# Expert-choice layer: full-precision tokens gathered per pair of experts, with four one-time places for expert 0's down weights

## The reference, cut to what matters

```python
def expert_choice_moe(xn, w_router, w_gate, w_up, w_down):
    cap = EC_CAPACITY_FACTOR * T // N_EXPERTS          # 32 tokens for each of 16 experts
    aff = jax.nn.softmax((xn @ w_router).astype(jnp.float32), axis=-1)
    g, idx = lax.top_k(jnp.swapaxes(aff, 1, 2), cap)
    xs = xn[bidx, idx]                                 # 32 x 1024 for each expert
    hid = jax.nn.silu(jnp.einsum('becd,edf->becf', xs, w_gate)) * jnp.einsum('becd,edf->becf', xs, w_up)
    y = jnp.einsum('becf,efd->becd', hid, w_down) * g[..., None].astype(xn.dtype)
    return jnp.zeros_like(xn).at[bidx, idx].add(y)
```

## Time and profile before

| what | us |
|---|---|
| device time, median of 3 runs | 2300.64 |
| lowest, highest | 2297.3, 2301.79 |
| profiled execution: its span, first to last instruction (the only time that its page gives) | 2299.6 |
| PE busy, PEld busy | 1914.4, 1382.4 |
| DVE busy, ACT busy, POOL busy | 913.0, 508.0, 30.6 |

### The profile page before, as it was taken

The page is one execution under the profiler, slowest core; times in us unless marked ns, Lnnn a source line. Parts: engine busy times, 40 slices in busy tenths (PEclk is TensorE's granted clock), DMA queues, the critical chain, the costliest instruction groups (busy, mean ns, idle before and its releaser), DMA issues.

```text
span 2299.6 us, 30109 instructions
## 1 busy us (share of the span) xinstructions
PE 1914.4 (83%) x13228; PEld 1382.4 (60%) x13228; DVE 913.0 (40%) x1242; ACT 508.0 (22%) x517; POOL 30.6 (1%) x23
## 2 busy tenths in 40 slices
PE   7999999999999999999999997556556665666565
PEld 7998789999999889999768672111111111111112
DVE  6788468556678647654346630000000000000001
ACT  4554023333455212333231120000000000000001
POOL 0000000000000010000000000000000000000000
PEclk9999999999999999999999979888887778788887
DMA  7444625556544634556524259999999999999996
GB/s 262 161 147 147 247 75 189 186 158 190 184 147 147 233 125 143 160 176 170 197 83 146 88 219 424 427 427 428 428 428 428 428 428 428 428 428 428 428 427 268
DMA packets 190182, 613.21 MB, mean 267 GB/s; under 512 B 8252, under 2 KB 106044, under 8 KB 164796
## 3 DMA queue, kind: packets, MB, share of 16 engines
q1 hardware_dynamic: 187712, 602.04, 67.7%
q10 hardware_dynamic: 2364, 9.58, 1.1%
HBM read 610.55 MB, written 1.05 MB: 266 GB/s over the span
## 4 chain that ended last, share of the span: by engine, by line
PE 53%; DMA 36%; DVE 8%; ACT 1%; issue 1%; SPq 0%; DVEq 0%; ACTq 0%; PEldq 0%
DMA work<-in_w_down 13%; DMA work<-in_w_gate 11%; DMA work<-in_w_up 11%; PE PS L1694 8%; PE PS L1687 8%; PE PS L1689 8%; PE PS L687 5%; PE PS L1621 3%; PE PS L925 2%; DVE ring_low L2396 1%; PE PS L941 1%; PE PS L1603 1%; PE PS L1717 1%; PE PS L1711 1%; PE PS L1712 1%
## 5 line engine op out<-in xcount | busy, mean ns | idle before, releaser
L925 PE MATMUL PS<-work,proj 128*32 128x512 f32 x1024 | 153.6, 734 | 99.0 <-DMA work<-in_w_up 64.3
L1449 DVE TENSOR_TENSOR proj<-proj,PS 128x512 f32<-128x512 f32 x16 | 11.0, 687 | 488.8 <-PE PS L925 488.8
L925 PE MATMUL PS<-ring,proj 128*32 128x512 f32 x768 | 116.1, 733 | 86.0 <-DMA ring<-in_w_up 49.9
L2147 ACT ACTIVATE high_f<-ring 128x4096 fp32r<-128x4096 f32 (+1 forms) x38 | 120.8, 3178 | 220.9 <-PE PS L1694 209.9
L2379 DVE TENSOR_TENSOR ring_low<-ring,high_f 128x4096 fp32r<-128x4096 f32 (+1 forms) x38 | 146.8, 3863 | 53.5 <-ACT high_f L2147 53.5
L925 PEld LDWEIGHTS PS<-work,proj 128*32 128x32 f32 x1024 | 31.1, 122 | 212.9 <-DMA work<-in_w_up 102.3
L1687 PE MATMUL PS<-xh_f,high_f 128*128 128x256 f32 x640 | 153.6, 280 | 0.3
L1689 PE MATMUL PS<-hT_low,high_f 128*128 128x256 f32 x624 | 151.1, 283 | 0.0
L687 PE MATMUL PS<-hT,ring 128*128 128x256 f32 (+1 forms) x576 | 130.4, 386 | 1.2 <-ACT hT L1068 1.2
L941 PE MATMUL PS<-work,proj 128*32 128x512 f32 x496 | 86.4, 831 | 49.8 <-DMA work<-in_w_down 46.4
L925 PEld LDWEIGHTS PS<-ring,proj 128*32 128x32 f32 x768 | 22.9, 121 | 172.6 <-DMA ring<-in_w_up 79.7
(11 more groups left out here) (527 smaller groups left out, 3702.6 us busy)
## 6 DMA issues: line engine op xcount, KB each, us to landing
ring<-in_w_in SPq DMA_DIRECT2D x73, 1024.0 KB, 7.3
work<-in_w_gate SPq DMA_DIRECT2D x33, 2048.0 KB, 35.7
work<-in_w_up SPq DMA_DIRECT2D x31, 2048.0 KB, 35.6
work<-in_w_down SPq DMA_DIRECT2D x31, 2048.0 KB, 35.7
ring<-in_w_up SPq DMA_DIRECT2D x25, 2048.0 KB, 35.6
ring<-in_w_gate SPq DMA_DIRECT2D x23, 2048.0 KB, 36.0
ring<-in_w_down SPq DMA_DIRECT2D x22, 2048.0 KB, 35.7
ring<-in_w_ada SPq DMA_DIRECT2D x24, 1024.0 KB, 7.3
```

The lines of the kernel that those rows point to most:

```text
L925: mm = nt.matmul(PS[32 * j:32 * j + 32, 2 + n // 4, :], x(k), w[:, F_E * kk + 512 * j:F_E * kk + 512 * (j + 1)], start=(k == 0), stop=(k = ...
L2147: na.activation(high(n)[:, w], ring[:, n % RING, w], ACT.Copy).then_inc(high_ready, 1)
```

## The change

Three things are changed together.

1. **Tokens.** They are kept once, in full 32-bit precision (TOK, written by the same four ACT instructions as `tok_high` before). `low_tokens` and its four DVE instructions are gone.
2. **Gather.** Only the 64 chosen places of a pair of experts are gathered at a time: 16 matmuls of 128 x 64 for each pair, all into bank 2, and one DVE addition over 128 x 512 (new `stage`) that writes XS of the pair. The first pair's gather stands ahead of expert 0; each later one stands on PE in the odd expert before it, between the turning of the hidden values and the down slots. PICK is rebuilt for each pair by two DVE comparisons of 128 x 64 from ROW, a copy of the row of token numbers. The ACT additions into XS (L1170) and the per-expert copies of DVE (L1439) are gone. All four zeroed bank pairs are opened in `route`, between the last turned tokens and the L898 matmul.
3. **Places.** The smaller tiles free blocks of `proj`, and `lora` and its neighbours are laid directly behind it. Expert 0's four down slots now each have a one-time place: `extra_a` (issued after `cat_ready` 1), `extra_b` (after `u2_ready` 4), the two halves in `con` and `hT` as before, and `extra_c` (after `ix_ready`). The ring's eight places hold its slots 0 to 7. The ring's own loads start again at m = 12, when PE has consumed expert 0's slot 0, and m = 20 waits for expert 1's slot 0.

The silu, product and result tiles share buffers (HE, YE on HSE; YE2 on HTE), and the squares of the router's norm use half the room. The numbers of the SP list after the first pair, the loop, the last expert's halves and everything behind them stay as they were.

The diff, cut to its core:

```diff
-PAIR, EXTRA = 2, 8
+PAIR, EXTRA, EXTRAS = 2, 8, 4
...
+        extra_a = proj[:, 8:24, :].rearrange("p a b -> p (a b)")
+        extra_b = nc.alloc_sbuf_tensor_at("extra_b", [P, SLOT], F32, offset=place["proj"] + 4 * 49 * T)
+        extra_c = proj[:, 33:49, :].rearrange("p a b -> p (a b)")
+        extra_halves = (con[:, 256:256 + SLOT // 2], hT[:, :, :].rearrange("p k t -> p (k t)"))
         def turn(m):
-            return m - 1
+            return m - EXTRAS
         def first_slot(m):
-            return m + 1 if m < EXTRA else m
+            return m + EXTRAS if m < EXTRA else m
...
+            first_load(0)
+            sp.wait_ge(block_done, BASE2 + 16)
+            first_load(1)
+            sp.wait_ge(cat_ready, 1)
+            sp.dma_start(extra_a, first_down(0).rearrange(whole, r=4)).then_inc(extra_a_full, 16)
+            sp.wait_ge(u2_ready, 2 * TT)
+            sp.dma_start(extra_b[:, :], first_down(1).rearrange(whole, r=4)).then_inc(extra_b_full, 16)
+            sp.wait_ge(yt_ready, 4)
+            for n in (2, 3, 4):
+                first_load(n)
+            sp.wait_ge(r_ss, 2)
+            first_load(5)
+            sp.wait_ge(block_done, BASE2 + 18)
+            first_load(6)
+            sp.wait_ge(block_done, BASE2 + 20)
+            first_load(7)
+            w = first_down(2).rearrange("(p h r) n -> h p (r n)", h=2, r=2)
+            for half, dst in enumerate(extra_halves):
+                sp.dma_start(dst, w[half]).then_inc(con_loaded, 16)
+            sp.wait_ge(ix_ready, 1)
+            sp.dma_start(extra_c, first_down(3).rearrange(whole, r=4)).then_inc(extra_c_full, 16)
+            for m in range(EXPERT_SLOTS, PAIR * EXPERT_SLOTS):
+                earlier = m - RING_E - EXTRAS if m < RING_E + EXPERT_SLOTS else m - RING_E
+                sp.wait_ge(expert_slots, EXPERT_SLOTS + earlier + 1)
+                sp.sem_inc(slot_freed, 1)
+                expert_load(m // EXPERT_SLOTS, m % EXPERT_SLOTS, m)
...
-                pe.wait_ge(topk_done, 1)
                 pe.wait_ge(dve2, 4)
-                zero_banks(YB[2:3])
+                zero_banks(YB[2:4])
+                pe.wait_ge(tok2_out, 4)
+                zero_banks(YB[0:2]).then_inc(scattered, 1)
                 pe.wait_ge(diag_ready, 1)
                 nt.matmul(PS[:, 3, :], ones[0:EXPERTS, :], DIAG[0:EXPERTS, :], ...).then_inc(row_ready, 1)
...
-                pe.wait_ge(tok2_low, 4)
+            def gather(first):
+                for k in range(KD):
+                    for t in range(TT):
+                        if first and k == 0:
+                            pe.wait_ge(pick_ready, t + 1)
+                        mm = nt.matmul(PS[:, 2, PAIR * CAP * k:PAIR * CAP * (k + 1)], TOK[:, t, 2 * P * (k // 2) + k % 2:2 * P * (k // 2 + 1):2],
+                                       PICK[:, t, :], start=(t == 0), stop=(t == TT - 1))
+                mm.then_inc(xs_psum, 1)
...
             def expert(e, pair, par):
-                pe.wait_ge(xs_staged, e)
+                if par == 0:
+                    pe.wait_ge(xs_out, pair + 1)
                 for n in range(8):
-                    hidden(staged, pair, EXPERT_SLOTS * par + n)
+                    hidden(staged(par), pair, EXPERT_SLOTS * par + n)
+                turned(e)
+                if par:
+                    pe.wait_ge(pick_ready, pair + 4)
+                    gather(False)
                 rest(e, pair, par)
             def first_expert():
-                gather(0, 4)
+                gather(True)
                 pe.wait_ge(ix_out, 1)
-                for n in range(4):
-                    if n in (1, 2):
-                        gather(2 * n + 2, 2 * n + 4)
-                    pe.wait_ge(xs_out, 2 * n + 2)
-                    hidden(first, 0, first_slot(n), n)
-                for n in range(4, 8):
-                    hidden(first, 0, first_slot(n), n)
-                zero_banks(YB[3:4] + YB[0:2]).then_inc(scattered, 1)
-                rest(0, 0, 0, True)
+                pe.wait_ge(xs_out, 1)
+                for n in range(8):
+                    if n == 4:
+                        pe.wait_ge(pick_ready, 3)
+                    hidden(staged(0), 0, first_slot(n), n)
+                turned(0)
+                down_extras()
+                pe.wait_ge(ye_ready, 2)
+                scatter(0, KD)
...
+                def pick(pair):
+                    for t in range(TT):
+                        ins = picked(t, ROW[:, bass.ts(pair, PAIR * CAP)])
+                    ins.then_inc(pick_ready, 1)
+                def stage(pair):
+                    dve.wait_ge(xs_psum, pair + 1)
+                    nv.tensor_tensor(XS, banks(2, 1, KD, PAIR * CAP), TOKEN_SHIFT.unsqueeze(2).broadcast_to([P, KD, PAIR * CAP]), ALU.add)\
+                        .then_inc(xs_out, 1)
...
+                with dve.Fori(1, EXPERTS // PAIR - 1) as pair:
+                    pick(pair + 1)
+                    gates(PAIR * pair)
+                    outputs(PAIR * pair)
+                    gates(PAIR * pair + 1)
+                    stage(pair + 1)
+                    outputs(PAIR * pair + 1)
```

More of the change, by code:

```diff
@@ L972, in scatter, with staged, rest @@
                 mm.then_inc(scattered, 1)
-            def rest(e, pair, par, with_extra=False):
-                turned(e)
+            def staged(par):
+                return lambda k: XS[:, k, CAP * par:CAP * (par + 1)]
+            def rest(e, pair, par):
                 for n in range(8, EXPERT_SLOTS):
[L978 to L981, removed]
+                    down(pair, EXPERT_SLOTS * par + n)
@@ L1013, in last_expert @@
                 for n in range(8):
-                    hidden(staged, pair, EXPERT_SLOTS + n)
+                    hidden(staged(1), pair, EXPERT_SLOTS + n)
                 turned(e)
@@ L1164, in second_scalar @@
                 act.wait_ge(tok2, i + 1)
[L1165 removed]
+                na.activation(TOK[:, t, 512 * g:512 * (g + 1)], PS[:, 4 + i, :], ACT.Identity, scale=N_STAT[:, t:t + 1]).then_inc(tok2_out, 1)
             act.wait_ge(ix_ready, 1)
[L1167 to L1170 removed]
+            na.activation(IG.rearrange("p a b -> p (a b)"), PS[:, 4, 0:32], ACT.Copy).then_inc(ix_out, 1)
             with act.Fori(0, EXPERTS) as e:
@@ L1418, in route, with picked @@
                 ins.then_inc(topk_done, 1)
-                low_tokens(1, 4)
                 dve.wait_ge(row_ready, 1)
                 for t in range(TT):
-                    nv.tensor_scalar(PICK[:, t, :], PS[:, 3, :], c3[:, D_TOK - D_WORK + t:D_TOK - D_WORK + t + 1], None, ALU.is_equal)\
-                        .then_inc(pick_ready, 1)
+                    picked(t, PS[:, 3, 0:PAIR * CAP]).then_inc(pick_ready, 1)
+                nv.tensor_copy(ROW, PS[:, 3, :]).then_inc(pick_ready, 1)
+            def picked(t, slots):
+                return nv.tensor_scalar(PICK[:, t, :], slots, c3[:, D_TOK - D_WORK + t:D_TOK - D_WORK + t + 1], None, ALU.is_equal)
             def gained(lo, hi):
@@ L1458, in experts @@
                 dve.wait_ge(ix_out, 1)
-                dve.wait_ge(xs_out, KD)
-                middle(0)
-                with dve.Fori(1, EXPERTS - 1) as e:
-                    stage(e)
-                    middle(e)
+                stage(0)
+                dve.wait_ge(pick_ready, 3)
+                pick(1)
+                gates(0)
+                outputs(0)
+                gates(1)
+                stage(1)
+                outputs(1)
+                with dve.Fori(1, EXPERTS // PAIR - 1) as pair:
[5 more added lines that the diff above has]
+                    outputs(PAIR * pair + 1)
                 last = EXPERTS - 1
-                stage(last)
+                gates(last - 1)
+                outputs(last - 1)
                 gates(last)
```

125 lines of the change are left out of this document (43 added, 82 removed).

## The result

| | before | after |
|---|---|---|
| device time, median, same chip, us | 2301.22 (4 runs, 2297.3 to 2302.89) | 2278.62 (4 runs, 2276.05 to 2280.54) |
| ratio, 95% interval | 1 | 0.9906 [0.9889, 0.9922] |
| profiled span, us | 2299.6 | 2277.2 |

The change takes 22.6 us off (17.9 to 25.5 by the interval of the ratio). The forecast was 16 us, 2284.6, and its lower end, 2281.5, lies above what was measured: faster, as foreseen, but by more than any case in it gives.

What follows compares the result with a forecast made beforehand. Layers were taken as bound by PE, experts by the DMA weight stream. Span 2299.6 less 14.7 (three slots) and 1.35 (earlier restart) gave 2283.55, or 2284.6 us device time; range 2281.5 to 2292.5.

Steps and rivals of the forecast that it cites:

- Sign: Whole kernel: faster, chance 0.96; same 0.01, slower 0.03.
- main term: Expert stream after the restart: 180 slots loaded instead of 183, 3 x 4.90 = 14.7 us less.
- The places: Ahead of the restart: the three early loads lie in idle DMA time and delay nothing later on SP.
- The restart: Between router and expert 0's slot 0: the expert loads start again at 1374.9 instead of 1376.23 us, 1.35 us gained.
- early zeros: In route ahead of L898: zero banks raise the clock early, ending between 1364.9 and 1366.1 us; L898 starts at 1365.6.
- Rival 1: First pair's gather in route: the clock holds at full, restart at 1374.15 us, time 2283.8 us; chance 0.25.
- Rival 2: Route: the clock stays at half, zeros delay L898 and the gather is slow, 2292.8 us; chance 0.12.
- Rival 3: Early loads: not all places save; one slot lost gives 2289.5 us (chance 0.04), none saved 2299.3 us (0.01).
- Rival 4: After expert 0: the stream runs dry, 53.5 us against 40.9, 12.6 us dry, 2305.4 us with rival 2; chance 0.03.
- The loop: Expert loop: each pair adds a 4.2 to 7.4 us gather on PE, hidden behind the stream; costs nothing.

Runs made afterwards that it cites:

- second measurement: The changed kernel, unaltered, timed again beside the layout runs on one chip: 2277.73 us, ratio 0.9908.
- late-zeros kernel: Changed kernel with three of the four zeroed bank pairs opened after expert 0's hidden slots instead of in route: 2282.58 us, ratio 0.9926.
- three relatives: Changed kernel without its three new early loads (2293.01 us), with a 16-byte shim ahead of `proj` (2281.47), and with a 64-byte one (2273.74).
- kernel with one place: Changed kernel without the three new early loads, expert 0's down weights 1 to 3 coming through the ring: 2293.01 us, ratio 0.9972.

## Why the prediction was right and wrong

- **Sign and main term: right.** Three slots fewer behind the restart, 14.7 us: 15.0 in the segments, 14.4 and 15.3 by taking the places out. Over all profiles at 428 GB/s what follows the restart takes 921.2 to 923.7 us with one place (six) and 904.0 to 909.4 with four (seven), the middle values 14 us apart. The places cost nothing: `extra_a` and `extra_b` went out 5.37 us apart (foreseen 5.35), `extra_c` at 1358.70. That last one was foreseen near 1367, but counted from the `con` issue it came 15.5 us after, where the foreseen 1367.1 would be 17.3.
- **The step that failed: the sum has no term for the layout.** It took everything ahead of the router as unchanged, though the change lists `par`, `lora`, `solve_tmp` and a new `spare` in another order. The same instructions in the new order are 5.0 us faster (2.5 to 6.7), and in that order the change gives 16.9 us (some 4 either way) where 16 was foreseen; 5.0 and 16.9 are the 21.9 of the second measurement. So the miss of 6.0 us is the layout's 5.0 and 1 us that is within what the runs of one kernel differ by.
- **The restart: the mechanism right, its gain of 1.35 us not shown.** The row (L917) took 1.12 us and the indices (L920) 0.51, against 1.04 and 0.45; the timeline of PE in the changed kernel and the stretches below it (columns as in rows 2) show the rest. The clock was at full speed when the row began and fell inside the gather while PE was busy 2.00 of 2.00 us; slot 0 at the half clock took 3.64.

```profile
1351.87 4.62 PE L886 MATMUL PS<-con,proj 128*128 128x256 f32 x16
1357.20 1.12 PE L917 MATMUL PS<-proj,con 16*128 16x512 f32 x2 [0.70 <-DVE proj L1427]
...
1358.70 5.47 PE L930 MATMUL PS<-cond,proj 128*128 128x64 f32 x32
1365.07 3.64 PE L941 MATMUL PS<-tri,proj 128*32 128x512 f32 x16 [0.90 <-issue]
```

```profile
1356.00:1358.00 2.00, 1.30 (x5) 0.57 (x4) 1.35 (x5) 0.00 (x0) 0.00 (x0) 1.00 0.00 0
...
1360.00:1362.00 2.00, 2.00 (x14) 2.00 (x14) 0.00 (x0) 0.21 (x1) 0.00 (x0) 0.68 0.65 246
1362.00:1364.00 2.00, 2.00 (x11) 1.98 (x10) 0.00 (x0) 0.00 (x0) 0.00 (x0) 0.50 1.01 434
...
1370.00:1372.00 2.00, 2.00 (x20) 0.63 (x16) 0.00 (x0) 0.00 (x0) 0.00 (x0) 0.76 0.73 262
```

  The forecast had 4.2 for the gather and the middle of 1.92 and 3.41 for the slot; 5.47 and 3.64 are 2.2 us more. The row began 14.0 us after the `con` issue instead of 15.8 in return, so that the segment came out at 25.64 (and 25.05 the second time) where 25.06 was foreseen. That two errors cancel is luck. The earlier row isn't the change's own either: in the new layout the old instructions begin theirs 14.1 us after the `con` issue (L899 at 1359.43).

  Nor can the 0.8 us of the table be credited to the change. From the `con` issue to the restart seven profiles of the old instructions took 24.86 to 26.42 us, ten with the new ones and the zeros early 22.43 to 26.68; in one layout it was 24.86 with the old instructions and 25.64 and 25.05 with the new. The zero banks (L886) took 4.62 us and ended ahead of the row, which then waited for DVE. In the late-zeros kernel the segment is 4.1 to 4.7 us longer, outside both ranges. So the early zeros are what keeps the new route level with the old one: the forecast had them at no cost, and the expectation for that run at a gain of only 1.5.
- **Rival 1, the clock holds,** came true in the profiles of three relatives (22.43, 22.44 and 22.43 us), not in the changed kernel's own two. **Rival 2,** the half clock throughout, came nearest to true with the zeros late (29.75 us, 3.3 more than before). Neither was the reason for the miss.
- **Rival 3** is out by the kernel with one place. **Rival 4,** the stream running dry after expert 0, is out too: `tri` for m = 20 went out at 1398.34, 29.5 us after the restart (28.9 foreseen, 40.9 allowed). Of the seven loads between, the first came 2.91 us after the restart and the others 1.7 us apart (1.77 foreseen for all). The GB/s from there on stay flat:

```profile
1380.00:1416.00 36.00, 29.41 (x232) 9.93 (x224) 2.94 (x5) 2.48 (x3) 0.00 (x0) 0.95 1.01 428
1416.00:1500.00 84.00, 57.42 (x340) 21.78 (x344) 5.24 (x11) 4.36 (x5) 0.00 (x0) 0.82 1.01 427
1500.00:2250.00 750.00, 484.67 (x2892) 160.03 (x2884) 35.13 (x65) 32.41 (x40) 0.00 (x0) 0.80 1.01 428
```

- **The loop: right.** A pair's gather costs PE up to 6.37 us. That one, at 2120.99, does stand in the chain of waits, but ahead of a load that then takes 35.37 us from issue to landing, behind the others. The stream shows no dip, so the end didn't wait for it.

What stays open is why a block's position changes PE's pace and the stream's rate. That both go with it is shown; the mechanism isn't. Nor is it shown where most of the layout's gain ahead of the router arises.

## What to carry to other kernels

A change that moves buffers carries a second change, the layout, and it was worth almost a third of the first here (5.0 us against 16.9): time the old instructions in the new layout before crediting the rest. When a stream sets the end, count slots behind its restart; that term came out within a few per cent. Work that nobody waits for, put into an idle stretch of PE ahead of a serial step, was worth 4 to 5 us here, and the rows show the higher granted clock that came with it.

## What was new about the hardware

- The start of `work` in SBUF set the rate of the expert stream: 431 GB/s at 96 bytes past a multiple of 128 (five profiles of five), 428 at 0, 32, 48, 64 and 80 (thirteen of thirteen). Only the loads into `work` and `tri` took less time (4.84 to 4.85 us between landings in place of 4.89 to 4.90); those into `ring`, which never moved, stayed at 4.88 to 4.89. A shim of 16 bytes took 10 us (0.4 to 0.5%) off the kernel before.
- In the feed-forward's down product, at the full clock and with PE never idle, 50 us held 420 and 421 matmuls in one layout and 426 in another.
- A gather of 16 matmuls, 32 records of 128x64, took 3.98 us at the full clock and 7.09 at the half one. The granted clock fell to 0.50 while such matmuls ran back to back (2.00 of 2.00 us busy).
